# One core, bidirectional encoder: row statistics of the first sequence from its transposed copy, and a new order of loads and small steps in the opening

## The reference, cut to what matters

```python
mod = jnp.dot(jax.nn.silu(c), w_ada) + b_ada
shift1, scale1, ... = jnp.split(mod, N_MOD, axis=-1)
h = (_rmsnorm(x, g_mix) * (1.0 + scale1) + shift1)
proj = jnp.einsum('bsd,de->bse', h, w_in)
log_g_f = jax.nn.log_sigmoid(ret_decay_f)      # 8 numbers, and 8 for the other direction
```

## Time and profile before

| what | us |
|---|---|
| median of 3 runs | 2536.96 (2535.18 to 2540.32) |
| profiled execution | 2539.32 |
| its span | 2537.2 |
| TensorE busy in the span | 2501.3 (99%) |
| VectorE, ScalarE, GpSimd busy | 1826.8, 1176.1, 1742.2 |

### The profile page before, as it was taken

How to read it: one execution, slowest core, us unless ns; L and a number is a source line. 1 busy time by engine, 2 the same in 40 slices (tenths; PEclk the granted TensorE clock), 3 DMA queues, 4 the chain that set the end, 5 groups by cost and what they waited for, 6 DMA issues and landing times.

```text
span 2537.2 us, 34984 instructions
## 1 busy us (share of the span) xinstructions
PE 2501.3 (99%) x12740; PEld 2105.4 (83%) x12740; DVE 1826.8 (72%) x2189; ACT 1176.1 (46%) x1818; POOL 1742.2 (69%) x1172
## 2 busy tenths in 40 slices
PE   6999999999999999999999999999999999999998
PEld 4889898988788888888888989898888888888887
DVE  4989888887886666755869898887679655656336
ACT  5433333335745545555634333333465545545443
POOL 1787777757487777654767978786565877775544
PEclk9999999999999999999999999999999999999999
DMA  9124242447055445597632515151532333336764
GB/s 337 42 86 137 86 138 86 154 162 238 20 174 174 147 156 174 172 360 222 191 111 67 163 49 176 42 164 62 192 100 63 109 95 108 109 95 209 194 193 151
DMA packets 297161, 362.15 MB, mean 143 GB/s; under 512 B 17440, under 2 KB 180640, under 8 KB 296992
## 3 DMA queue, kind: packets, MB, share of 16 engines
q1 hardware_dynamic: 292960, 348.39, 43.1%
q10 hardware_dynamic: 4032, 11.54, 1.3%
HBM read 283.84 MB, written 75.50 MB: 142 GB/s over the span
## 4 chain that ended last, share of the span: by engine, by line
PE 91%; DVE 4%; POOL 2%; ACT 1%; issue 1%; SPq 0%; DMA 0%; DVEq 0%; POOLq 0%; ACTq 0%
PE ps L1137 29%; PE ps L1604 17%; PE ps L1311 16%; PE ps L1536 10%; PE ps L1198 5%; PE ps L1555 3%; PE ps L1445 3%; PE ps L1242 2%; PE ps L1391 1%; PE ps L1658 1%; PE ps L1648 1%; PE ps L1649 1%; PE ps L1623 1%; PE ps L1634 1%; DVE hc_lo L2647 0%
## 5 line engine op out<-in xcount | busy, mean ns | idle before, releaser
L2391 POOL TENSOR_TENSOR f_w<-f_ring,f_w 128x512 fp32r<-128x512 f32 x434 | 592.2, 1371 | 384.2 <-ACT f_w L1940 381.0
L1137 PE MATMUL ps<-hc_hi,f_w 128*128 128x512 f32 x2240 | 690.3, 389 | 1.2 <-DVE u_lin L2662 0.5
L2314 POOL TENSOR_TENSOR f_w<-f_ring,f_w 128x512 fp32r<-128x512 f32 x282 | 462.6, 1652 | 241.1 <-ACT f_w L1727 240.6
L1137 PEld LDWEIGHTS ps<-hc_hi,f_w 128*128 128x128 f32 x2240 | 420.0, 188 | 90.5 <-ACT u_act L2002 1.7
L1137 PE MATMUL ps<-hc_lo,f_w 128*128 128x512 f32 x1120 | 435.8, 389 | 0.0
L1311 PE MATMUL ps<-act_ring,f_w 128*128 128x512 f32 x1812 | 411.9, 389 | 0.0
L1311 PEld LDWEIGHTS ps<-act_ring,f_w 128*128 128x128 f32 x1812 | 339.9, 188 | 70.5
L1940 ACT ACTIVATE f_w<-f_ring 128x512 fp32r<-128x512 f32 x434 | 269.6, 623 | 235.2 <-POOL f_ring L2401 105.3
L1604 PE MATMUL ps<-hb,f_w 128*128 128x512 f32 x1440 | 347.4, 395 | 0.0
L1727 ACT ACTIVATE f_w<-f_ring 128x512 fp32r<-128x512 f32 x282 | 175.9, 627 | 323.4 <-POOL f_ring L2322 137.0
L1604 PEld LDWEIGHTS ps<-hb,f_w 128*128 128x128 f32 x1440 | 268.3, 188 | 61.3 <-issue 6.7
(11 more groups left out here) (263 smaller groups left out, 4076.2 us busy)
## 6 DMA issues: line engine op xcount, KB each, us to landing
f_ring<-in_w_in SPq DMA_DIRECT2D x176, 256.0 KB, 4.5
f_ring<-in_w_up SPq DMA_DIRECT2D x160, 256.0 KB, 3.4
f_ring<-gated_out SPq DMA_DIRECT2D x152, 256.0 KB, 3.0
late_rows<-in_w_late SPq DMA_DIRECT2D x64, 512.0 KB, 4.1
gated_out<-gated_up SPq DMA_DIRECT2D x44, 512.0 KB, 3.8
f_ring<-down_sums SPq DMA_DIRECT2D x88, 256.0 KB, 3.0
gated_out<-t_gated SPq DMA_DIRECT2D x22, 768.0 KB, 5.4
f_ring<-in_w_down SPq DMA_DIRECT2D x66, 256.0 KB, 3.5
```

Of the source, the lines that this page charges most:

```text
L1137: ins = pe.matmul(ps_row[:, half_of(bank)], a[:, cols], b, start=i in (0, 1, 3) and k == 0 and n == 0, stop=k == KQ - 1 and n == 2, skip_g ...
L2314: pool.tensor_tensor(out[:, 1, :], raw, out[:, 0, :].bitcast(F32), ALU.subtract).then_inc(mix_lo.sem, 1)
L2391: pool.tensor_tensor(piece_slot(q)[:, 1, :], piece_raw(q), piece_slot(q)[:, 0, :].bitcast(F32), ALU.subtract).then_inc(piece_lo.sem, 1)
```

## The change

Token-order tiles of the first sequence are not loaded any more. The turned chunks come in halves: tokens 0 to 511 of all eight by ScalarE's queue at once, tokens 512 to 1023 by SyncE behind the first weights. ScalarE squares each half chunk (128 by 512). For the first half GpSimd adds the eight squares in seven additions, for the second VectorE does. TensorE multiplies the sum by a column of ones (four matmuls with one column each), VectorE adds epsilon, GpSimd takes the root as before.

SyncE issues the first eight `w_ada` tiles directly behind two small loads; the decay loads come behind them and two weight pieces. VectorE's decay steps are cut into four stretches that stand between the first pieces. On TensorE all eight products of the second modulation part stand behind n = 16, with the sums of the second half behind the second of them and the spreading behind the fifth.

```diff
-            for half, src in enumerate((decay_f, decay_b)):
-                sp.dma_start(lg..., src.partition_broadcast(P)).then_inc(decay_in, 16)
-            sp.dma_start(cst[:, C_ID + P:C_ALL], ...).then_inc(decay_in, 16)
...
-            for k in range(KQ):
+            for k in range(KC):
                 early_tile(0, k)
             for j in range(2):
                 mix_in(mix0, j)
-            for k in range(KQ, KC):
-                early_tile(0, k)
-            turned_chunk(0)
-            turned_chunk(1)
-            second_tile(4)
-            second_tile(5)
-            turned_chunk(2)
+            for half, src in enumerate((decay_f, decay_b)):
+                sp.dma_start(lg..., src.partition_broadcast(P)).then_inc(decay_in, 16)
+            sp.dma_start(cst[:, C_ID + P:C_ALL], ...).then_inc(decay_in, 16)
             for j in range(2, 4):
                 mix_in(mix0, j)
-            second_tile(6)
-            second_tile(7)
-            turned_chunk(3)
+            for k in range(KC):
+                turned_half(k)
...
+            def squares_of_x(half):
+                pe.wait_ge(*x_low.at(first, (KC - 1) * (half + 1)))
+                for t in range(4):
+                    col = 6 * HALF + t
+                    ins = pe.matmul(ps_row[:, col:col + 1], x_sq[:, 0, t * P:(t + 1) * P], ones[:, 0:1], start=True, stop=True)
+                ins.then_inc(x_stat.sem, 1)
             for k in range(KC):
                 early_product(0, k)
                 if k == 4:
-                    spread_rstd(first, (0,))
+                    squares_of_x(0)
+            spread_rstd(first, (0,))
             ada_turn(0)
...
-                    if n == 14:
-                        spread_rstd(first, (1,))
                     if n == 16:
+                        for k in range(KC):
+                            early_product(1, k)
+                            if k == 1:
+                                squares_of_x(1)
+                            if k == 4:
+                                spread_rstd(first, (1,))
                         pe.wait_ge(*rrow_done.at(first, 2))
-                    if n in range(12, 20):
-                        early_product(1, n - 12)
```

More of the change, by code:

```diff
@@ L2074, in _ @@
             modulate_piece(first, 0, 0, 8, 1)
+            act.wait_ge(table_step, 1)
+            act.activation(small[:, 1, :], small[:, 0, :], ACT.Exp, scale=-1.0).then_inc(table_act, 1)
             mix_high(mix0, 2)
             mix_high(mix0, 3)
-            square_x(first, 4)
+            square_first(1, 0)
             modulate_piece(first, 0, 0, 8, 2)
-            square_x(first, 5)
-            square_x(first, 6)
-            square_x(first, 7)
+            square_first(1, 1)
+            square_first(1, 2)
             modulate_piece(first, 0, 0, 8, 3)
+            for k in range(3, KC):
+                square_first(1, k)
+            act.wait_ge(table_args, 1)
+            act.activation(pairT[:, :, 0:T_GAIN], pairT[:, :, 0:T_GAIN], ACT.Exp).then_inc(table_act, 1)
             row_factors(first, 1)
@@ L2430, in _ @@
             first = ("first", 0, 0)
+            for n, dst, other in Y_SUMS:
+                pool.wait_ge(*x_squared.at(first, other + 1))
+                if n:
+                    pool.wait_ge(*x_low.at(first, n))
+                pool.tensor_tensor(x_sq[:, dst, :], x_sq[:, dst, :], x_sq[:, other, :], ALU.add).then_inc(x_low.sem, 1)
             for half in range(2):
                 tiles = slice(4 * half, 4 * half + 4)
-                pool.wait_ge(*x_squared.at(first, 4 * half + 4))
-                pool.tensor_scalar(x_ms[:, tiles], x_ms[:, tiles], EPS, None, ALU.add).then_inc(x_eps.sem, 1)
                 pool.wait_ge(*x_eps.at(first, half + 1))
@@ L2573, in norm_scale @@
                 k, begin, end = pieces[where[0]][i]
-                dve.wait_ge(*xt_in[k].at(where, 16))
+                if where[0] == "first" and begin == 0:
+                    dve.wait_ge(*x_in[k].at(where, 16))
+                if where[0] == "swap" or end == S:
+                    dve.wait_ge(*xt_in[k].at(where, 16))
                 at_k = xT[seq][:, k, begin:end]
@@ L2783, in _ @@
-            step(dve.tensor_tensor(small[:, 4, :], small[:, 3, :], small[:, 3, :], ALU.mult))
-            step(dve.tensor_scalar(small[:, 5, :], small[:, 4, :], 1.0 / 17, None, ALU.mult))
-            for k in range(7, 0, -1):
-                step(dve.scalar_tensor_tensor(small[:, 5, :], small[:, 5, :], 1.0 / (2 * k + 1), small[:, 4, :],
-                                              ALU.add, ALU.mult))
-            step(dve.scalar_tensor_tensor(small[:, 5, :], small[:, 5, :], 1.0, small[:, 3, :], ALU.add, ALU.mult))
@@ L2789, in _ @@
-            step(dve.tensor_scalar(small[:, 0, :], logit, 0.0, None, ALU.min))
-            step(dve.scalar_tensor_tensor(logit, small[:, 5, :], -2.0, small[:, 0, :], ALU.mult, ALU.add))
-            for d in range(2):
-                pos = cst[:, C_POS + d:C_POS + d + 1]
-                dve.tensor_scalar(pairT[:, :, T_DK + d:T_DK + 4:2], lg[:, d, :, :], pos, None, ALU.mult)
-            for d in range(2):
-                half = slice(d * DK, (d + 1) * DK)
-                dve.tensor_scalar(pairT[half, :, T_DC:T_DC + 2], lg[half, d, :, :], float(P), None, ALU.mult)
@@ new lines, in decay_series @@
+            def decay_series():
+                for k in range(7, 0, -1):
+                    step(dve.scalar_tensor_tensor(small[:, 5, :], small[:, 5, :], 1.0 / (2 * k + 1), small[:, 4, :],
+                                                  ALU.add, ALU.mult))
+                step(dve.scalar_tensor_tensor(small[:, 5, :], small[:, 5, :], 1.0, small[:, 3, :], ALU.add, ALU.mult))
+                step(dve.tensor_scalar(small[:, 0, :], logit, 0.0, None, ALU.min))
+                step(dve.scalar_tensor_tensor(logit, small[:, 5, :], -2.0, small[:, 0, :], ALU.mult, ALU.add))
@@ new lines, in decay_gains, with mean_of_x @@
+            def decay_gains():
+                dve.wait_ge(table_act, 2)
+                dve.tensor_scalar(pairT[:, :, T_DK:T_DK + 4], pairT[:, :, T_DK:T_DK + 4], K_SCALE, None, ALU.mult)
+                for col, row, factor in ((T_GAIN, R_GAIN, 0.25), (T_PS, R_PS, 0.5)):
+                    step(dve.tensor_scalar(pairT[:, :, col:col + 2], vecT[:, row:row + 8].rearrange("p (a b) -> p a b", b=2),
+                                           factor, None, ALU.mult))
+            def mean_of_x(half):
+                dve.wait_ge(*x_stat.at(first, half + 1))
+                dve.tensor_scalar(x_ms[:, 4 * half:4 * half + 4], ps_row[:, 6 * HALF:6 * HALF + 4], EPS,
+                                  None, ALU.add).then_inc(x_eps.sem, 1)
@@ L2813, in copy_ada, with add_late_squares @@
+            def add_late_squares(n):
+                _, dst, other = X_SUMS[n]
+                dve.wait_ge(*x_squared.at(first, KC + other + 1))
+                if n:
+                    dve.wait_ge(*x_low.at(first, KC - 1 + n))
+                dve.tensor_tensor(x_sq[:, dst, :], x_sq[:, dst, :], x_sq[:, other, :], ALU.add).then_inc(x_low.sem, 1)
+            mean_of_x(0)
             def copy_ada(part):
```

108 lines of the change are left out of this document (54 added, 54 removed).

## The result

The changed kernel took 2544.64 us (median of 8 runs, 2540.39 to 2546.24) against 2537.41 us for the kernel before (8 runs, 2535.18 to 2540.32). The ratio is 1.0025, with a 95% interval of 1.0017 to 1.0034: slower by 7.2 us, outside the predicted range (2532.5 to 2540.0) and not on the side of the forecast, 2536.5. The profiled execution took 2546.24 us, its span 2544.4 (before 2537.2).

The account below looks back on a forecast made before the run. The prediction took TensorE as the bound, busy 2501.3 of 2537.2 us. A at 27.5 plus 27.85 put B at 55.35 against 55.78, 0.4 us gained: 2536.96 - 0.4 = 2536.5 us, range 2532.5 to 2540.0.

Parts of the forecast that it names:

- only what TensorE waits for in the opening counts: Opening: a change there can win only TensorE's idle time, 36 us in all, if what follows moves up too.
- B: Start of step n = 23, first to use piece 7: 55.78 us before, predicted 55.35; its shift taken as the whole's.
- H: Start of the first matmul behind the projection, not named in the prediction: 84.46 us before, 84.0 by its gain.
- Loads and the first row factors: Opening up to the modulation: eighth w_ada tile landed at 20.0, GpSimd's additions over at 17.2, modulation ready at 24.5 or 25.5.
- A: First projection matmul: 29.16 us before, predicted 27.5 within 26.2 to 28.3, so 1.7 earlier.
- n = 1 to 16: First projection steps behind A: 48 matmuls in 13.2 us, with VectorE's decay steps, additions and low parts keeping up.
- From n = 16 to n = 17: Products, ones, mean, root, spreading and ladder in one row behind n = 16; n = 17 at A + 21.3.
- From n = 17 to B: Pieces 5 and 6, the turn, then 2.75 us from turn to B: 3.8 + 2.75 us.
- Behind B: Rest of the projection: 126 matmuls in 28.84 us without a gap, unchanged because the code is the same.
- Rival 3: VectorE bounds A to n = 16, additions at 1.67 to 1.77 us: 5.6 to 6.3 us lost; chance 0.07.
- Rival 1: TensorE at 2.4 GHz when A comes: n = 1 to 16 in 11.0 us, gain 3.9, 2533.1 us; chance 0.13.
- Rival 2: Wait on GpSimd replaces the transfer: additions of 1.75 us put A at 30, cost 2 us, 2539.0; chance 0.08.

Follow-up runs that it names:

- all_mended: Changed kernel with stat_early's second-half statistics at n = 13 and 15, first additions on VectorE, weight piece 1's high part early, and three further reorderings; ratio 1.0008.
- before_both: Kernel before with products_only's edit, piece 7's low part ahead of second bias, gain and scale 8, and second ada copy ahead of that; 2534.24 us, ratio 0.9992.
- x_only: Changed kernel with the decay loads back ahead of w_ada in SyncE's queue and all decay steps in one block ahead of the first mean; ratio 1.0023.
- spread_only: Kernel before with the spreading of the second row factors moved from n = 14 to behind n = 16, products left in place; ratio 1.0020.
- mix45_early: Changed kernel with the splitting of weight pieces 4 and 5 moved ahead of the second half's row factors and root; ratio 1.0018.
- fill_clock: Changed kernel with added matmuls that compute nothing, 20 behind the first turn and 16 ahead of n = 23, to keep TensorE busy; ratio 1.0024.
- products_only: Kernel before with the eight products of the second modulation part grouped behind n = 16, the spreading left at n = 14; ratio 0.9993.
- decays_act: Changed kernel with the small decay loads on ScalarE's queue and all decay steps ahead of the first mean, the Exp behind the squares; ratio 1.0035.
- before_grouped: Kernel before with the eight second-part products grouped behind n = 16 and the spreading behind the fifth of them; ratio 1.0015.
- stat_early: Changed kernel with second-half sums at n = 13, spreading at n = 15, eight products behind n = 16, and VectorE's decay series and arguments behind the mean; ratio 1.0019.
- mix1_early: Changed kernel with ScalarE making the high part of weight piece 1 before it copies the first row factors; ratio 1.0021.
- dve_first: Changed kernel with the seven additions of the first half's squares on VectorE in place of GpSimd; ratio 1.002.
- best_turn: Changed kernel with stat_early, dve_first, mix1_early and mix45_early joined, and the second ada result turned at n = 20 instead of 21; ratio 1.0001.

## Why the prediction was wrong, point by point

**That only what TensorE waits for in the opening counts, and that a shift there is the shift of the whole.** Right, with one error of place: B was not the last point. The same 126 matmuls took 1.6 us more behind a B that TensorE had waited 3.6 us for (predicted: no change), and H can be held by VectorE though B is early (`all_mended`, `before_both`).

**Loads and the first row factors (A 27.5, measured 30.76).** This step failed by the size of its terms. The last first half of x landed at 15.9 instead of 13.0: the engines moved 338 GB/s from 3 to 10 us and not 387, and of its 2.10 MB ScalarE's queue had moved 1.90 by 13.0, so the last packets came late. Why they did, no run tests. The eighth `w_ada` tile landed at 21.2 instead of 20.0, but TensorE didn't wait for it. GpSimd's additions cost the predicted 1.28 each, but the last four came back to back from 13.98 to 19.49, where 17.2 was said. The four matmuls against ones took 1.87, not 1.1, at the low clock. And gain took 0.97, not 0.17. From the modulation to A it took 2.5 (2.8 predicted).

**n = 1 to 16 (13.2 us, measured 14.2).** The step that failed is the one that asked whether the others keep up. It priced the decay steps at 0.17 to 0.25 each and left out that they stand ahead of a low part and beside `mix_low` 2 and 3; `x_only`, without them, took 13.2. VectorE's additions themselves were right at 0.69 each, and the last was over in time.

**From n = 16 to n = 17 (8.1 us, measured 8.3).** Right in every link: products 1.00, ones 0.98, spreading 1.10, row factors 0.61, scale 0.70, ScalarE's pair 1.5. `spread_only` shows the price of this step alone, 3.7 us; the prediction had +3.3 for it.

**From n = 17 to B (6.55 us, measured 8.29).** This step failed by a wait that it left out: gain and the low part of piece 7 sit out GpSimd's subtractions. With the clock behind B, which follows from it, it costs 3.3 us against the forecast, as much as A. Either alone would have left the time at about 2539.8, just inside the range; both together put it outside. With `mix_low` 4 and 5 out of the way this stretch took 6.40 (`mix45_early`). The prediction took the ladder from the kernel before, where gain started just as `mix_low` 5 was ending. These two rows of the kernel before would have told it:

```profile
51.22 2.54 POOL L2314 TENSOR_TENSOR f_w<-f_ring,f_w 128x512 fp32r<-128x512 f32 x2 [12.47 <-ACT f_w L1727]
...
53.73 0.17 DVE L2851 SCALAR_TENSOR_TENSOR modT<-modT,vecT 128x8 f32<-128x8 f32 x1
```

The subtractions end at 53.76. I had moved VectorE's steps against GpSimd's without asking what GpSimd does beside them.

**Behind B (28.84, measured 30.42).** The clock after the longer wait. The clock was asked about only at A, and that the matmuls behind B would run as before was taken from their being the same code.

In a sum, at H: A 3.3, n = 1 to 16 1.0, the ladder 0.2, n = 17 to B 1.7, the clock 1.6, together 7.8, and from the predicted 84.0 to 91.84 it is 7.8.

**The rivals.** Rival 3 had the right mechanism and the right price (a step that meets a subtraction sits it out, up to 1.28 us) in the wrong place: I looked for it at the additions ahead of `squares_of_x(1)`, where it did not decide, and gave it 0.07. It acted on single small steps on the path: at gain for A, at gain and low part for B. Rival 1 was wrong, since VectorE sets the pace to n = 16 (`fill_clock`). Its sum, 2542.1 to 2542.8, took A's gain off twice where it said "less what A gained". Rival 2 (additions of 1.75) didn't happen, though the additions on GpSimd did end later and A came near its 30. That nearly all "hidden" steps had slack was right in the mean and wrong at the two points where the whole kernel hangs on one row of VectorE.

## What to carry to other kernels

When a step moves, look at every engine's row beside its new place, not only at the one that runs it: a 0.17 us instruction on the critical ladder took 1.0 us because another engine's subtraction had begun 0.3 us ahead of it. A chain of handovers to TensorE (here spreading to first matmul, 3.8 us) wants independent matmuls behind its first link, not ahead of it; `spread_only` and `products_only` are the same work and differ by 7.3 us at the end, some 2.5 of it the low clock behind the longer wait. And before moving work out of a wait into a later stretch, see which engine is nearly full there (VectorE 27.3 of 30 us here).

## What the runs showed of the hardware that I had not expected

- The size of an instruction says nothing of what it loses beside GpSimd: a 128 x 16 step went from 0.17 to 1.15 us, a series of seven from 1.43 to 4.40, a low part from 0.69 to 1.75, and GpSimd's own pair of subtractions from 2.54 to 3.56 where VectorE came first. A step with one operand in SBUF lost as much (1.21) as those with two.
- The granted clock fell to 0.50 behind several of TensorE's waits, and the length of the wait alone doesn't tell which: it fell behind all of 3.6 to 3.8 us ahead of n = 17 or B (the kernel after, `decays_act`, `before_grouped`, `stat_early`, `spread_only`). Of the waits of 2.4 us ahead of n = 17 it fell behind those of `mix1_early`, `dve_first`, `fill_clock` and `x_only`, and not behind the same wait in the kernel after and `mix45_early`; it fell behind one of 2.0 us in `best_turn` and not behind one of 2.7 in `products_only`. So kernels with the same wait paid for the low clock in different places.
